# Gathered expert rows as whole rows of 8 KB in two buffers, with one VectorE operation of 2048 columns each, in place of half rows of 4 KB in three buffers

## The chip, the cores and the metric

One core of one Trainium2 chip runs the whole program. The metric is the device time of one execution in microseconds (us), the median over several runs. A profiled execution gives, besides its own time, the span from its first to its last instruction.

## What is computed

One block of a model over 256 tokens of width 2048, in fp32. A first half (RMSNorm, one input projection, differential attention and a gated MLP group, an output projection, residual) is not touched. The second half is a PEER expert layer: each token scores 16384 experts through product keys, keeps 16 of them for each of 8 heads, and sums their value rows with gated, activated weights. The reference, cut to what matters:

```python
def one_block(xb):                      # xb: (128 tokens, 2048)
    q = (xb @ w_q).reshape(T, 8, 2, 128)
    sc = jnp.einsum('thcd,hckd->thck', q, sub_keys)
    s1, i1 = lax.top_k(sc[:, :, 0], 16)
    s2, i2 = lax.top_k(sc[:, :, 1], 16)
    cand = (s1[..., :, None] + s2[..., None, :]).reshape(T, 8, 256)
    best, ci = lax.top_k(cand, 16)
    e1 = jnp.take_along_axis(i1, ci // 16, axis=-1)
    e2 = jnp.take_along_axis(i2, ci % 16, axis=-1)
    idx = e1 * 128 + e2                 # 128 picks per token
    g = jax.nn.softmax(best, axis=-1)
    act = jax.nn.gelu(jnp.einsum('td,thkd->thk', xb, u_tab[idx]))
    return jnp.einsum('thk,thkd->td', g * act, v_tab[idx])
```

`u_tab` and `v_tab` are two tables of 16384 rows of 2048 fp32 values, 8 KB a row.

## The kernel before

The expert layer is done in two ways at once. For 208 of the 256 tokens the kernel multiplies with both tables in full on TensorE: a **score stage** over `u_t` (128 steps of two units, 256 units of 512 KB each, called n below) and a **value stage** over `peer_v` (256 units, called v or u). In each unit ScalarE copies the loaded 512 KB into a rounded high part `HI` (L674), VectorE, or GpSimd in some plain steps, subtracts it from the raw data to get the low part (L1136 in the score stage, L445 on GpSimd, L1129 for two units at once in the value stage), and TensorE multiplies high with high and low (L1557, L1597) and low with high (L1563, L1602). TensorE's instructions for unit n are eight high products, then the eight low products of unit n-1. SyncE loads the units (L376) into a ring of 6 slots in the score stage and of 10 in the value stage; a slot is loaded again once the low products of the unit in it have been done.

The other 48 tokens are the **gathered tokens**. Each of their 48 x 128 picks is one row of `peer_u` and one of `peer_v`. With 128 picks on the 128 partitions, they make NG = 48 groups for each table: 32 groups for the first 32 tokens, 16 for the last 16. GpSimd fetches a group by an indirect DMA (L454) into a buffer `PICKED`, with the row numbers in `PK4`. VectorE then multiplies the rows with the tokens' input and sums them to one dot product per partition (L1190, with a small instruction that reads the accumulator), or in the value stage multiplies them by their weight and adds them to `ACC4` or `ACC8` (L1198, L1195 for the first). Each group is handled as two halves of 1024 columns, so there are 192 indirect DMAs and 192 VectorE operations. Three half buffers are in turn: gather k waits until VectorE has done operation k-3.

The order of the work is written out by hand, the same for all engines. What sets it around the change:

- In a score step j VectorE does, in this order: the sum of the two halves of PSUM (`sum_halves`, L1145), the low parts of units 2j+4 and 2j+5, some pieces of the choice of experts (top-k, one-hots and sums; `PIECE_COUNT`, up to step 56), from step 60 to 111 the one-hots and gates, and then a row operation if j is in the list `HALF_STEPS`. These are steps 40, 43, ..., 58, then every second step from 60 to 110, then every step from 112 to 120: 42 operations.
- In the value stage VectorE does for each even u the low part of the weights (L1205) and of two units of values (L1129), and a row operation if u is in `HALF_UNITS`: 150 operations on units 9 to 248, some 1.6 units apart.
- GpSimd goes through the same steps: a low part where one is its own, then the gathers that have become free. After the score stage it loads `X8` (L482) with the last 16 tokens' input, and late in the value stage it issues twelve loads for the end of the kernel (L492), one behind each gather.

GpSimd's row numbers come from VectorE: `SPK` is made from the picked experts (L1105 to L1108), saved to memory and read back as `PK4`. Since the halves are rows of a table of 32768 half rows, the number is doubled, and the second half's is that plus one:

```python
link(v.tensor_scalar(SPK[:, 0, :], SPK[:, 0, :], 1, None, ALU.logical_shift_left))
v.tensor_scalar(SPK[:, 1, :], SPK[:, 0, :], 1, None, ALU.bitwise_or)
```

Of the kernel before, what the change touches and what calls it, by code (L numbers as in the profile page):

```python
# [14 lines left out]
P = 128  # L15
# [35 lines left out]
ROW_SLOTS = 3  # L51
# [51 lines left out]
HALF_UNITS = [FREE_UNITS[i * len(FREE_UNITS) // (HALVES - len(HALF_STEPS))] for i in range(HALVES - len(HALF_STEPS))]  # L103
LAST_DOT = HALF_UNITS[2 * NG - 1 - len(HALF_STEPS)]
FIRST_B_DOT = HALF_UNITS[2 * GROUPS_A - len(HALF_STEPS)]
FIRST_B_SUM = HALF_UNITS[2 * NG + 2 * GROUPS_A - len(HALF_STEPS)]
SEL_A_AT = 2 * NKEYS - 4
assert 0 < FIRST_B_DOT and LAST_DOT < NKEYS - 1 and FIRST_B_SUM >= NKEYS + 62
GATHERED = {j: (ROW_SLOTS if j >= ROWS_BACK_AT else 0) + sum(i < j for i in HALF_STEPS) for j in range(NKEYS)}
# [25 lines left out]
def hybrid_peer_block(nc, x, w_in, w_out, wq_t, keys_t, u_t, peer_u, peer_v, ws_t, bs_t, gain_t, ffn_gain, z_gain,  # L135
                      final_gain, lambdas, rope, out):
    ctx = ExitStack()
    with ctx:  # L138
# [42 lines left out]
        SPK = at("SPK", 94 * KB, [P, 3, PICKS], U32)  # L181
# [25 lines left out]
        PICKED = [at("PICKED0", 192 * KB, [P, HALF]), at("PICKED1", 196 * KB, [P, HALF]), at("PICKED2", 104 * KB, [P, HALF])]  # L207
        PK4 = at("PK4", 108 * KB, [P, 3, NG], U32)
# [29 lines left out]
        DOTS = small("DOTS", [P, 2, NG])  # L238
# [5 lines left out]
        spk_dram = nc.dram_tensor("spk_spill", [NS, 3, PICKS], U32).ap()  # L244
# [43 lines left out]
        halves, dots, dots_gelu, sel_ready = sem("halves"), sem("dots"), sem("dots_gelu"), sem("sel_ready")  # L288
# [98 lines left out]
        def _(pool):  # L387
# [89 lines left out]
            for k in range(GATHERED[NKEYS - 1], len(HALF_STEPS) + ROW_SLOTS):  # L477
                gather(k)
# [8 lines left out]
            for k in range(len(HALF_STEPS) + ROW_SLOTS, HALVES):  # L487
                gather(k)
                if HALF_UNITS[k - ROW_SLOTS - len(HALF_STEPS)] >= NKEYS + 50 and late:
# [11 lines left out]
        def _(act):  # L501
# [258 lines left out]
            for v in range(N_V):  # L760
# [4 lines left out]
                if v == LAST_DOT:  # L765
                    act.wait_ge(dots, 1)
                    nc.scalar.activation(DOTS[:, 0, :], DOTS[:, 0, :], ACT.Gelu_apprx_tanh).then_inc(dots_gelu, 1)
# [31 lines left out]
        def _(dve):  # L799
# [260 lines left out]
            def choice(o):  # L1060
# [116 lines left out]
            def half_rows(k):  # L1177

                half = k % 2
                g = k % (2 * NG) // 2  # L1180
                cols = slice(half * HALF, (half + 1) * HALF)
                rows = PICKED[k % ROW_SLOTS][:]
                dve.wait_ge(row_ready[k % ROW_SLOTS], 16 * (k // ROW_SLOTS + 1))
                if k < 2 * NG:
                    if k == 0:
                        dve.wait_ge(x4_ready, 16 * (P // NA))
                    if k == 2 * GROUPS_A:
# [518 lines left out]
```

## Time and profile before

| | us |
|---|---|
| median of 3 runs | 1778.72 (1778.35 to 1779.86) |
| profiled execution, its own time | 1775.03 |
| its span, first to last instruction | 1772.9 |
| TensorE busy | 1743.1, 98% of the span |
| VectorE busy | 1424.3, 80% |
| ScalarE busy | 931.0, 53% |
| GpSimd busy | 410.6, 23% |
| granted TensorE clock, mean | 0.998 |

The score stage runs from 454 to 1129 us of the span, the value stage from 1130 to 1757 us. Busy times are unions of the instructions' durations; PE is TensorE's matmuls, PEld its weight loads, DVE is VectorE, ACT ScalarE, POOL GpSimd, SPq the queue of SyncE that issues loads. The idle time given in a row is that of the engine just before the instruction, with the instruction that ended it.

### The profile page before, as it was taken

To read this page: it belongs to the slowest core of one execution; us is meant where nothing else is said; L and a number is where in the kernel's file an instruction comes from. 1 tells how busy PE (TensorE), PEld (TensorE's weight loads), DVE (VectorE), ACT (ScalarE), POOL (GpSimd) and SP (SyncE) were. 2 spreads that over 40 slices of the span, in tenths; PEclk is the share of its full clock that TensorE was granted. 3 is DMA by queue.
4 is the path that set the end of the run, shared out by engine and by line. 5 is a ranking of instruction groups with operands and counts; after the bars stand their busy time and mean duration, and the time that the engine had idled before them with its cause. 6 is when DMAs were issued, how large, how long until landed. Compare 5 with 4: busy or idle time off the path is not lost. (4 is left out here: it accounts for less than half of the span.)

```text
span 1772.9 us, 28848 instructions
## 1 busy us (share of the span) xinstructions
PE 1743.1 (98%) x10950; PEld 1653.4 (93%) x10950; DVE 1424.3 (80%) x2151; ACT 931.0 (53%) x1400; POOL 410.6 (23%) x294
## 2 busy tenths in 40 slices
PE   9999999999999999999999999999999999999997
PEld 7887778778999999999999999999999999999997
DVE  5545786475579899999999998588888998888995
ACT  5444564453456554555555555555555555555553
POOL 0002300020142133111111112023433333343331
PEclk9999999999999999999999999999999999999999
DMA  7665445677566677777677778899999999999992
GB/s 245 210 183 161 143 148 170 193 234 237 175 219 218 218 256 243 248 244 228 227 231 231 233 233 314 256 335 367 353 359 356 354 321 356 365 363 405 368 349 91
DMA packets 127026, 462.59 MB, mean 261 GB/s; under 512 B 14736, under 2 KB 14832, under 8 KB 126240
## 3 DMA queue, kind: packets, MB, share of 16 engines
q1 hardware_dynamic: 95760, 347.65, 59.0%
q0 software_dynamic: 30992, 112.67, 17.1%
q8 instruction: 84, 1.38, 0.3%
q10 hardware_dynamic: 144, 0.52, 0.1%
q14 instruction: 46, 0.38, 0.1%
HBM read 455.73 MB, written 5.05 MB: 260 GB/s over the span
## 5 line engine op out<-in xcount | busy, mean ns | idle before, releaser
L1597 PE MATMUL PS<-W,HI 128*128 128x416 f32 x2048 | 436.9, 353 | 2.1 <-ACT HI L674 1.4
L1557 PE MATMUL PS<-xT,HI 128*128 128x416 f32 x2048 | 438.1, 356 | 0.0
L674 ACT ACTIVATE HI<-V_RAW 128x1024 fp32r<-128x1024 f32 x256 | 271.6, 1061 | 284.1 <-PE PS L1597 152.2
L1597 PEld LDWEIGHTS PS<-W,HI 128*128 128x128 f32 x2048 | 365.0, 189 | 7.2 <-ACT HI L674 1.6
L1557 PEld LDWEIGHTS PS<-xT,HI 128*128 128x128 f32 x2048 | 365.8, 189 | 2.3
L1129 DVE TENSOR_TENSOR V_LO<-V_RAW,HI 128x2048 fp32r<-128x2048 f32 x128 | 293.0, 2289 | 59.7 <-ACT HI L674 53.5
L674 ACT ACTIVATE HI<-RING_RAW 128x1024 fp32r<-128x1024 f32 x256 | 269.5, 1053 | 50.8 <-DMA RING_RAW<-u_t 49.7
L1136 DVE TENSOR_TENSOR RING_LO<-RING_RAW,HI 128x1024 fp32r<-128x1024 f32 x232 | 274.6, 1218 | 6.8 <-ACT HI L674 6.7
L811 DVE TENSOR_TENSOR LO<-RAW,HI 128x1024 fp32r<-128x1024 f32 x132 | 163.0, 1237 | 136.4 <-PE PS L1330 99.9
L1563 PEld LDWEIGHTS PS<-xT,RING_LO 128*128 128x128 f32 x2048 | 268.3, 191 | 4.1 <-DVE RING_LO L1136 2.0
L1602 PEld LDWEIGHTS PS<-W,V_LO 128*128 128x128 f32 x2048 | 269.3, 191 | 1.9 <-DVE V_LO L1129 0.9
L1602 PE MATMUL PS<-W,V_LO 128*128 128x208 f32 x2048 | 268.3, 272 | 0.5 <-DVE V_LO L1129 0.5
L1563 PE MATMUL PS<-xT,RING_LO 128*128 128x208 f32 x2048 | 266.9, 273 | 1.3 <-DVE RING_LO L1136 1.3
L454 POOL DMA_INDIRECT PICKED<-peer_u,PK x96 | 146.4, 1525 | 492.6 <-DVE DOTS L1190 484.3
L504 ACT ACTIVATE HI<-RAW 128x1024 fp32r<-128x1024 f32 x144 | 152.7, 1065 | 156.1 <-DMA RAW<-wq_t 47.4
L454 POOL DMA_INDIRECT PICKED<-peer_v,PK x96 | 134.5, 1401 | 234.3 <-DVE ACC L1198 202.6
L1325 PE MATMUL PS<-HI,xT 128*128 128x512 f32 x440 | 139.3, 398 | 2.5 <-ACT HI L504 1.8
L1330 PE MATMUL PS<-HI,xT 128*128 128x512 f32 x440 | 136.0, 390 | 0.0
L707 ACT ACTIVATE HOLES<-PS 128x208 f32<-128x208 f32 x128 | 44.1, 345 | 153.3 <-PE PS L1563 151.3
L1198 DVE SCALAR_TENSOR_TENSOR ACC<-PICKED,DOTS,ACC 128x1024 f32<-128x1024 f32 x92 | 116.5, 1279 | 9.2 <-DMA PICKED<-peer_v,PK 9.1
L1190 DVE CUSTOM_DVE_ANT_0 PICKED<-PICKED,X 128x1024 f32<-128x1024 f32 x96 | 116.4, 1219 | 6.6 <-DMA PICKED<-peer_u,PK 4.8
L1330 PEld LDWEIGHTS PS<-HI,xT 128*128 128x128 f32 x440 | 82.6, 188 | 17.6
(207 smaller groups left out, 1656.4 us busy)
## 6 DMA issues: line engine op xcount, KB each, us to landing
RING_RAW<-u_t SPq DMA_DIRECT2D x256, 512.0 KB
V_RAW<-peer_v SPq DMA_DIRECT2D x256, 512.0 KB
RAW<-w_in SPq DMA_DIRECT2D x80, 512.0 KB, 3.6
RAW<-w_out SPq DMA_DIRECT2D x32, 512.0 KB, 4.3
RAW<-wq_t SPq DMA_DIRECT2D x32, 512.0 KB, 4.8
x_spill<-X POOLq DMA_DIRECT2D x2, 1024.0 KB, 5.3
X1R<-x_spill POOLq DMA_DIRECT2D x8, 256.0 KB
X<-x SPq DMA_DIRECT2D x3, 512.0 KB, 8.4
```

The lines of the kernel that those rows point to most:

```text
L454: pool.indirect_dma_start(PICKED[k % ROW_SLOTS][:], None, table.rearrange("e (a c) -> (e a) c", a=2), bass.IndirectOffsetOnAxis(PK4[:, hal ...
L504: nc.scalar.activation(HI[:, slot, :], RAW[:, slot, :], ACT.Copy).then_inc(hi_ready, 1)
L674: nc.scalar.activation(HI[:, n % HI_SLOTS, :], raw_of(n), ACT.Copy).then_inc(top_ready, 1)
L811: v.tensor_tensor(LO[:, u % 2, :], RAW[:, u % 4, :], HI[:, u % 4, :].bitcast(FP32), ALU.subtract).then_inc(lo_ready[u % 2], 1)
L1129: nc.vector.tensor_tensor(pair_of(V_LO, v), pair_of(V_RAW, v), HI[:, slot:slot + 2, :].bitcast(FP32), ALU.subtract)\
L1136: v.tensor_tensor(low_of(n), raw_of(n), HI[:, n % HI_SLOTS, :].bitcast(FP32), ALU.subtract).then_inc(low_dve, 1)
L1325: mm(banks[c], high(tt), h[:, halves[c]], start=first, stop=False)
L1330: ins = mm(banks[c], low(tt), h[:, halves[c]], start=False, stop=last and tt > 0)
L1557: return mm(PS[:, j % S_BANKS, 0:2 * ND].rearrange("p (a t) -> p a t", a=2), HI[:, n % HI_SLOTS, kk * P:(kk + 1) * P], xT[:, k, :, 0:ND], ...
L1563: return mm(PS[:, j % S_BANKS, 0:ND], low_of(n)[:, kk * P:(kk + 1) * P], xT[:, k, 0, 0:ND], start=False, stop=k == KT - 1)
L1597: return mm(PS[:, V_BANKS[i], 0:2 * ND].rearrange("p (a t) -> p a t", a=2), HI[:, v % HI_SLOTS, i * P:(i + 1) * P], weights_of(v), start=v ...
L1602: return mm(PS[:, V_BANKS[i], 0:ND], low_of(N_U + v)[:, i * P:(i + 1) * P], weights_of(v)[:, 0, :], start=False, stop=v % NKEYS == NKEYS - 1)
```

## The change

A group's 128 rows are fetched whole, by one indirect DMA of 8 KB for each row. There are two buffers of 8 KB a partition instead of three of 4 KB, so gather k waits for operation k-2. A row operation works on 2048 columns; there are 96 of them and 96 gathers. `ROW_STEPS` are 40, 46, 52, 58, then every fourth step from 60 to 108, then 112, 114, ..., 120: 22 operations. `ROW_UNITS` are 74 units from 9 to 246, some 3.2 apart. The two instructions that double the row numbers go, and so does the addition of the two halves' dot products; `SPK` and `PK4` have two planes instead of three. The last operation on `peer_u` rows signals `dots` itself. In the value stage an operation adds to the accumulator that the operation before it wrote, so it waits for that one (`rows_done >= k`), where before it waited for the last but one.

```diff
-ROW_SLOTS = 3
+ROW_SLOTS = 2
...
-HALVES = 4 * NG
-HALF_STEPS = list(range(40, SPREAD0, 3)) + list(range(SPREAD0, SPREAD_END, 2)) + list(range(SPREAD_END, NKEYS - 7))
+ROW_STEPS = list(range(40, SPREAD0, 6)) + list(range(SPREAD0, SPREAD_END, 4)) + list(range(SPREAD_END, NKEYS - 7, 2))
...
-        PICKED = [at("PICKED0", 192 * KB, [P, HALF]), at("PICKED1", 196 * KB, [P, HALF]), at("PICKED2", 104 * KB, [P, HALF])]
-        PK4 = at("PK4", 108 * KB, [P, 3, NG], U32)
+        PICKED = [at("PICKED0", 192 * KB, [P, D]), at("PICKED1", 104 * KB, [P, D])]
...
             def gather(k):
 
-                table = peer_u if k < 2 * NG else peer_v
-                g, half = k % (2 * NG) // 2, k % 2
                 if k >= ROW_SLOTS:
-                    pool.wait_ge(halves, k - ROW_SLOTS + 1)
-                pool.indirect_dma_start(PICKED[k % ROW_SLOTS][:], None,
-                                        table.rearrange("e (a c) -> (e a) c", a=2),
-                                        bass.IndirectOffsetOnAxis(PK4[:, half, g:g + 1], 0))\
+                    pool.wait_ge(rows_done, k - ROW_SLOTS + 1)
+                pool.indirect_dma_start(PICKED[k % ROW_SLOTS][:], None, peer_u if k < NG else peer_v,
+                                        bass.IndirectOffsetOnAxis(PK4[:, 0, k % NG:k % NG + 1], 0))\
                     .then_inc(row_ready[k % ROW_SLOTS], 16)
...
-                    link(v.tensor_scalar(SPK[:, 0, :], SPK[:, 0, :], 1, None, ALU.logical_shift_left))
-                    v.tensor_scalar(SPK[:, 1, :], SPK[:, 0, :], 1, None, ALU.bitwise_or)
-                    v.tensor_copy(SPK[:, 2, :].bitcast(FP32), ROWS[:, 2]).then_inc(spk, 1)
+                    v.tensor_copy(SPK[:, 1, :].bitcast(FP32), ROWS[:, 2]).then_inc(spk, 1)
...
-            def half_rows(k):
+            def full_rows(k):
...
-                    ins = v.tensor_tensor_reduce(rows, rows, x_rows[:, cols], 1.0, 0.0, ALU.mult, ALU.add,
-                                                 DOTS[:, half, g:g + 1])
+                    ins = v.tensor_tensor_reduce(rows, rows, x_rows[:], 1.0, 0.0, ALU.mult, ALU.add, DOTS[:, g:g + 1])
...
-                        dve.wait_ge(halves, k - 1)
-                        ins = v.scalar_tensor_tensor(acc, rows, DOTS[:, 0, g:g + 1], acc, ALU.mult, ALU.add)
-                ins.then_inc(halves, 1)
+                        dve.wait_ge(rows_done, k)
+                        ins = v.scalar_tensor_tensor(acc, rows, DOTS[:, g:g + 1], acc, ALU.mult, ALU.add)
+                ins.then_inc(dots if k == NG - 1 else rows_done, 1)
...
-                        v.tensor_tensor(DOTS[:, 0, :], DOTS[:, 0, :], DOTS[:, 1, :], ALU.add).then_inc(dots, 1)
```

On VectorE's queue in score step 43 there stands a row operation before. The rows are its pieces of the choice (`CAND`, `BEST`), the row operation (`PICKED`), and the start of step 44. Before:

```order
L1057 MAX BEST<-CAND 128x8
L1058 MAX_INDEX CI<-BEST,CAND 128x8
L1190 ISA PICKED_101,DOTS<-PICKED_101,X_95 128x1024
L1190 ISA DOTS 128x1
L1145 TENSOR_TENSOR store<-PS,HOLES 128x208
L1136 TENSOR_TENSOR RING_LO<-RING_RAW,HI 128x1024
```

Now, in the same place:

```order
L1051 MAX_INDEX CI<-BEST,CAND 128x8
L1052 MATCH_REPLACE CAND<-BEST,CAND 128x256
L1053 MAX BEST<-CAND 128x8
L1054 MAX_INDEX CI<-BEST,CAND 128x8
L1139 TENSOR_TENSOR store<-PS,HOLES 128x208
L1130 TENSOR_TENSOR RING_LO<-RING_RAW,HI 128x1024
```

The half row operation of step 43 is gone; steps 49 and 55 lose theirs in the same way.

At the end of score step 46 and the start of step 47, VectorE before:

```order
L1089 CAST CF<-CIA 128x128
L1190 ISA PICKED_102,DOTS<-PICKED_102,X_95 128x1024
L1190 ISA DOTS 128x1
L1145 TENSOR_TENSOR store<-PS,HOLES 128x208
L1136 TENSOR_TENSOR RING_LO<-RING_RAW,HI 128x1024 x2
```

Now:

```order
L1085 CAST CF<-CIA 128x128
L1182 ISA PICKED_101,DOTS<-PICKED_101,X_95 128x2048
L1182 ISA DOTS 128x1
L1139 TENSOR_TENSOR store<-PS,HOLES 128x208
L1130 TENSOR_TENSOR RING_LO<-RING_RAW,HI 128x1024 x2
```

The operation in this place has twice the columns, and it is the second of the stage where it was the third; steps 40, 52 and 58 change likewise.

## Rows read from the trace of the kernel before

**Rows 1.** The page, part 1: busy us, share of the span, instructions

```profile
PE 1743.1 (98%) x10950; PEld 1653.4 (93%) x10950; DVE 1424.3 (80%) x2151; ACT 931.0 (53%) x1400; POOL 410.6 (23%) x294
```

**Rows 2.** Waits of PEld, 454 to 1773 us: total us, times, longest us

```profile
PEld PS L1563 <- DVE RING_LO L1136: 2.0, 2, 1.1
PEld PS L1597 <- ACT HI L674: 1.6, 1, 1.6
...
PEld PS L1602 <- DVE V_LO L1129: 0.9, 1, 0.9
```

**Rows 3.** Timeline of PEld, 680 to 710 us: start us, us, what [idle before]

```profile
689.00 1.44 PEld L1557 LDWEIGHTS PS<-xT,HI 128*128 128x128 f32 x8
...
691.41 1.44 PEld L1557 LDWEIGHTS PS<-xT,HI 128*128 128x128 f32 x8
693.91 0.97 PEld L1563 LDWEIGHTS PS<-xT,RING_LO 128*128 128x128 f32 x8 [1.07 <-DVE RING_LO L1136]
...
702.10 1.44 PEld L1557 LDWEIGHTS PS<-xT,HI 128*128 128x128 f32 x8
704.50 0.97 PEld L1563 LDWEIGHTS PS<-xT,RING_LO 128*128 128x128 f32 x8 [0.96 <-DVE RING_LO L1136]
```

**Rows 4.** Window 692 to 703 us: us, then PE, PEld, DVE, ACT, POOL busy

```profile
692.00:703.00 11.00, 10.29 (x68) 9.74 (x67) 10.62 (x28) 5.01 (x8) 2.40 (x1) 1.00 0.74 251
```

**Rows 5.** The page, part 5: groups, count | busy us, mean ns | idle before

```profile
L1129 DVE TENSOR_TENSOR V_LO<-V_RAW,HI 128x2048 fp32r<-128x2048 f32 x128 | 293.0, 2289 | 59.7 <-ACT HI L674 53.5
...
L454 POOL DMA_INDIRECT PICKED<-peer_u,PK x96 | 146.4, 1525 | 492.6 <-DVE DOTS L1190 484.3
...
L1198 DVE SCALAR_TENSOR_TENSOR ACC<-PICKED,DOTS,ACC 128x1024 f32<-128x1024 f32 x92 | 116.5, 1279 | 9.2 <-DMA PICKED<-peer_v,PK 9.1
L1190 DVE CUSTOM_DVE_ANT_0 PICKED<-PICKED,X 128x1024 f32<-128x1024 f32 x96 | 116.4, 1219 | 6.6 <-DMA PICKED<-peer_u,PK 4.8
```

**Rows 6.** Timeline of DVE near 685 and 1340 us

```profile
685.00 1.28 DVE L1190 CUSTOM_DVE_ANT_0 PICKED<-PICKED,X 128x1024 f32<-128x1024 f32 x1
...
686.20 0.36 DVE L1145 TENSOR_TENSOR store<-PS,HOLES 128x208 f32<-128x208 f32 x1
...
1339.06 2.29 DVE L1129 TENSOR_TENSOR V_LO<-V_RAW,HI 128x2048 fp32r<-128x2048 f32 x1
1341.26 1.22 DVE L1190 CUSTOM_DVE_ANT_0 PICKED<-PICKED,X 128x1024 f32<-128x1024 f32 x1
...
1342.40 0.58 DVE L1205 TENSOR_TENSOR W<-store,W 128x416 fp32r<-128x416 f32 x1
```

**Rows 7.** Timelines of POOL, SP, ACT and PEld, 1103 to 1120 us

```profile
1103.36 1.96 POOL L454 DMA_INDIRECT PICKED<-peer_u,PK  x1 [4.89 <-DVE DOTS L1190]
...
1104.82 0.33 SPq L376 DMA_DIRECT2D RING_RAW<-u_t  x1
...
1112.07 1.06 ACT L674 ACTIVATE HI<-RING_RAW 128x1024 fp32r<-128x1024 f32 x1 [2.97 <-DMA RING_RAW<-u_t]
...
1119.36 1.06 ACT L674 ACTIVATE HI<-RING_RAW 128x1024 fp32r<-128x1024 f32 x1 [0.91 <-DMA RING_RAW<-u_t]
...
1114.18 1.44 PEld L1557 LDWEIGHTS PS<-xT,HI 128*128 128x128 f32 x8
```

**Rows 8.** Window 1109 to 1110 us: ..., PEclk, DMA share, GB/s

```profile
1109.00:1110.00 1.00, 1.00 (x9) 1.00 (x8) 1.00 (x2) 0.10 (x1) 0.00 (x0) 1.00 1.00 393
```

**Rows 9.** Timeline of DVE, 1606 to 1622 us

```profile
1609.08 1.28 DVE L1198 SCALAR_TENSOR_TENSOR ACC<-PICKED,DOTS,ACC 128x1024 f32<-128x1024 f32 x1 [1.28 <-DMA PICKED<-peer_v,PK]
1612.96 1.29 DVE L1198 SCALAR_TENSOR_TENSOR ACC<-PICKED,DOTS,ACC 128x1024 f32<-128x1024 f32 x1 [2.59 <-DMA PICKED<-peer_v,PK]
```

**Rows 10.** Timeline of DVE near 615 and 808 us: two sums and their idle time

```profile
614.61 0.38 DVE L1145 TENSOR_TENSOR store<-PS,HOLES 128x208 f32<-128x208 f32 x1 [0.80 <-ACT HOLES L707]
...
807.73 0.38 DVE L1145 TENSOR_TENSOR TMP<-PS,HOLES 128x208 f32<-128x208 f32 x1 [0.63 <-ACT HOLES L707]
```

**Rows 11.** Timeline of PEld, 1142 to 1152 us

```profile
1147.27 1.44 PEld L1597 LDWEIGHTS PS<-W,HI 128*128 128x128 f32 x8 [1.59 <-ACT HI L674]
```

More of the change, by code:

```diff
@@ L96 @@
 PIECE_COUNT, PLAIN_STEP = piece_counts()
-HALVES = 4 * NG
-HALF_STEPS = list(range(40, SPREAD0, 3)) + list(range(SPREAD0, SPREAD_END, 2)) + list(range(SPREAD_END, NKEYS - 7))
+ROW_STEPS = list(range(40, SPREAD0, 6)) + list(range(SPREAD0, SPREAD_END, 4)) + list(range(SPREAD_END, NKEYS - 7, 2))
 FREE_UNITS = [u for u in range(9, 250) if u not in (NKEYS - 2, NKEYS - 1)]
[L103 to L106, printed above, removed]
+ROW_UNITS = [FREE_UNITS[i * len(FREE_UNITS) // (2 * NG - len(ROW_STEPS))] for i in range(2 * NG - len(ROW_STEPS))]
+LAST_DOT = ROW_UNITS[NG - 1 - len(ROW_STEPS)]
+FIRST_B_DOT = ROW_UNITS[GROUPS_A - len(ROW_STEPS)]
+FIRST_B_SUM = ROW_UNITS[NG + GROUPS_A - len(ROW_STEPS)]
 SEL_A_AT = 2 * NKEYS - 4
 assert 0 < FIRST_B_DOT and LAST_DOT < NKEYS - 1 and FIRST_B_SUM >= NKEYS + 62
-GATHERED = {j: (ROW_SLOTS if j >= ROWS_BACK_AT else 0) + sum(i < j for i in HALF_STEPS) for j in range(NKEYS)}
+GATHERED = {j: (ROW_SLOTS if j >= ROWS_BACK_AT else 0) + sum(i < j for i in ROW_STEPS) for j in range(NKEYS)}
 S_BANKS = 3
@@ L180, in hybrid_peer_block @@
         ROWS = at("ROWS", 92 * KB, [P, 3, PH * TOPK])
-        SPK = at("SPK", 94 * KB, [P, 3, PICKS], U32)
+        SPK = at("SPK", 94 * KB, [P, 2, PICKS], U32)
         KEYS = at("KEYS", 96 * KB, [P, HC, NKEYS])
@@ L237, in hybrid_peer_block @@
         TMP = small("TMP", [P, ND])
-        DOTS = small("DOTS", [P, 2, NG])
+        DOTS = small("DOTS", [P, NG])
+        PK4 = small("PK4", [P, 2, NG], U32)
         PS = ctx.enter_context(nc.psum_tensor("PS", [P, 8, BANK], FP32))
@@ L476, in _ @@
                     gather(k)
-            for k in range(GATHERED[NKEYS - 1], len(HALF_STEPS) + ROW_SLOTS):
+            for k in range(GATHERED[NKEYS - 1], len(ROW_STEPS) + ROW_SLOTS):
                 gather(k)
@@ L486, in _ @@
                      for c in range(D // BANK)]
-            for k in range(len(HALF_STEPS) + ROW_SLOTS, HALVES):
+            for k in range(len(ROW_STEPS) + ROW_SLOTS, 2 * NG):
                 gather(k)
-                if HALF_UNITS[k - ROW_SLOTS - len(HALF_STEPS)] >= NKEYS + 50 and late:
+                if ROW_UNITS[k - ROW_SLOTS - len(ROW_STEPS)] >= NKEYS + 50 and late:
                     pool.wait_ge(low_used, N_U + NKEYS + 44)
@@ L1175, in land @@
                 v.tensor_tensor(store[:, j, 0:t], store[:, j, 0:t], TMP[:, 0:t], ALU.mult).then_inc(landed, 1)
[L1177 to L1181 removed]
+            def full_rows(k):
+                g = k % NG
                 rows = PICKED[k % ROW_SLOTS][:]
                 dve.wait_ge(row_ready[k % ROW_SLOTS], 16 * (k // ROW_SLOTS + 1))
[L1184 removed]
+                if k < NG:
                     if k == 0:
                         dve.wait_ge(x4_ready, 16 * (P // NA))
[L1187 removed]
+                    if k == GROUPS_A:
                         dve.wait_ge(x8_ready, 16 * (P // NB_))
                     x_rows = X4 if g < GROUPS_A else X8
[L1190 to L1191 removed]
+                    ins = v.tensor_tensor_reduce(rows, rows, x_rows[:], 1.0, 0.0, ALU.mult, ALU.add, DOTS[:, g:g + 1])
                 else:
[L1193 removed]
+                    acc = (ACC4 if g < GROUPS_A else ACC8)[:]
                     if g in (0, GROUPS_A):
[L1195 removed]
+                        ins = v.tensor_scalar(acc, rows, DOTS[:, g:g + 1], None, ALU.mult)
                     else:
[L1197 to L1199 removed]
+                        dve.wait_ge(rows_done, k)
+                        ins = v.scalar_tensor_tensor(acc, rows, DOTS[:, g:g + 1], acc, ALU.mult, ALU.add)
+                ins.then_inc(dots if k == NG - 1 else rows_done, 1)
+                if k == NG - 1:
+                    dve.wait_ge(dots, 1)
+                    dve.sem_inc(rows_done, 1)
             def weights_lo(q):
@@ L1629, in last_unit @@
                         if i == 0:
-                            pe.wait_ge(halves, HALVES)
+                            pe.wait_ge(rows_done, 2 * NG)
                         ins = gathered_out(i, ACC8, SEL8, NA, NB_, True)
@@ L1657, in _ @@
                     pe.wait_ge(sel_ready, 2)
-                    pe.wait_ge(halves, HALVES - 2 * GROUPS_B)
+                    pe.wait_ge(rows_done, 2 * NG - GROUPS_B)
                     for i in range(DT):
```

24 lines of the change are left out of this document (10 added, 14 removed).

## The prediction, made before the changed kernel ran

> **What bounds the kernel.** I read the page's busy times first, then the waits of TensorE's weight loads in the two expert stages, then the timelines at the places where it waits. TensorE is busy for 98% of the span, VectorE for 80% [rows 1]. TensorE's weight loads come in units of 2.41 us, one unit starting at 689.00 and the next at 691.41 [rows 3]. What another engine costs the kernel is only what makes a unit longer, and there is little of that: 2.0 us in two waits for VectorE's `RING_LO` in the score stage, 1.6 us in one wait for ScalarE's `HI` and 0.9 us in one wait for `V_LO` at the start of the value stage [rows 2]. At 691.41 the eight high products start; they take 1.44 us, so the low ones should start at 692.85, and start at 693.91 [rows 3]. The other wait, at 704.50, is of the same kind and 0.96 us long. Around these two VectorE has no room: 10.62 us busy of 11 [rows 4]. They are in score steps 45 and 47, where the pieces of the choice and the row operations both lie.
>
> So the change can win at most 2.0 us in the score stage, plus the 2.5 us of waits in the value stage if those are its doing. It can lose wherever it makes VectorE or a load late by more than its margin.
>
> **VectorE's work.** A half row operation shows as 1219 ns on `peer_u` and 1279 ns on `peer_v`, and there are 192 of them with the four first ones [rows 5]. What counts is the distance from its start to the next start: 1.20 us at 685.00, 1.14 us at 1341.26 [rows 6]. A whole row operation is not in the trace. The nearest row is `V_LO`, two inputs and 2048 columns in fp32: 2289 ns [rows 5], 2.20 us from start to start [rows 6]. From below, nothing makes it less than one half (1.14); from above, it is at most two halves (2.3 to 2.4). I take 2.2, from the row with its very shape, for both kinds. The 96 pairs then shrink by about 0.1 us each, some 9 us of VectorE's time in all. Nearly all of it is worth nothing, since VectorE ends most steps by waiting for ScalarE or TensorE, as for 0.63 us at 807.73 in the gated steps and 0.80 us at 614.61 [rows 10], and in the value stage for `HI`, 53.5 us in sum [rows 5].
>
> **Where the lumps fall.** In steps 40 to 58 the half operations at 40, 43, 46 and so on become whole ones at 40, 46, 52, 58. Up to step 43's end VectorE is 2.2 - 1.15 = 1.05 us later than before, after it 0.1 us earlier. Up to the second stall (step 47) three half operations have run before (3.5 us, the 1.20 one included) and two whole ones now (4.4 us): VectorE is 0.9 us later just where TensorE already waited for it. VectorE has no idle time between to take this up [rows 4]. The waits therefore add up to 2.0 + 0.9 = 2.9 us instead of 2.0. Earlier, the 1.05 us meets small margins in steps 41 to 44 and makes a wait there; that is part of the 2.9 us and not added to it, since each wait moves TensorE back and gives VectorE time for the next. Once TensorE has slipped by 0.9 us, the later lumps (steps 52 and 58) put VectorE no later against it than before. **Term 1: +0.9 us.** Its bounds are -2.0 us, if the waits vanish, and +1.3 us, if a whole operation costs two halves.
>
> **Loads of the ring.** A gather now moves 1 MB at once instead of 512 KB, in the same bytes overall. In steps 112 to 120 this meets the ring of six slots. The unit whose load SyncE issues at 1104.82 is copied by ScalarE at 1112.07, 7.25 us later, after 2.97 us idle; a gather was issued at 1103.36. The copy is done at 1113.13 and TensorE starts on the unit at 1114.18, so 1.05 us were left [rows 7]. A later unit with no gather before it made ScalarE idle for 0.91 us [rows 7]. One gather of 512 KB so costs a load up to 2.06 us. The other 512 KB, if they move at the 393 GB/s of the busiest slice there [rows 8], take 1.3 us; less the margin of 1.05 us, 0.3 us of wait remain for that unit. There are five such gathers (after the operations of steps 112 to 120), and for most the margin is larger. From below this costs nothing (the gather and the load need not meet). From above each of the five costs 2.06 us more, 1.0 us over the margin, 5 us in sum. **Term 2: +0.5 us**, by the rate of the busiest slice, one or two gathers of the five.
>
> The Trainium skill's page "DMA: Bandwidth & Descriptors", section "Queues, rings and completion order", says that each DMA engine goes round the queues packet by packet and empties a whole packet, some 9 to 17 descriptors, before it turns to the next queue. With 8 rows of each gather on an engine that would let a load wait for a whole gather, now of twice the length, which is the first rival below. This trace has only the 2.06 us of one half gather.
>
> **GpSimd.** 96 indirect DMAs of about 1.5 us [rows 5] go, with as many waits. GpSimd had waited for VectorE for 484 us before them [rows 5], so nobody gains. Its low parts in steps 41 to 45 wait for VectorE's and move with term 1; the gather of step 44 no longer stands behind one of them. **Other edits**, each at nothing: the two instructions on `SPK` (about half a us) lie in step 30, and VectorE waits for `HOLES` in the next step [rows 10]; without that wait they would be worth their own length. The addition of the dot products is one small operation in the value stage, where VectorE has room. The wait for the operation just before the accumulation is free, as the two are some 3 units (7 us) apart. The twelve late loads go out over more units, end near unit 214 instead of 197, and are needed behind unit 255.
>
> **Value stage.** A pair of units lasts 4.8 us. With a whole row operation VectorE needs 2.2 for `V_LO`, 0.5 for the weights and 2.2 for the rows, 4.9 us, and in the pairs without one 2.7. It lags by 0.1 us and has it back in the next pair. Its margin there is large: near 1609 it lost 1.28 and 2.59 us in waiting for two gathers [rows 9], and no wait of TensorE answers to it [rows 2]. Two buffers of whole rows also give a gather more time, two intervals of 3.2 units against three of 1.6. The one wait of 1.59 us at 1147.27 [rows 11] falls before the first row operation of that stage, with no row gather under way, and behind the burst of `X8` and ring loads, so it stays. **Term 3: 0.**
>
> **Sum.** The profiled execution took 1775.03 us, 3.69 us under the median of 1778.72. Against its own time the change gives 1775.03 + 0.9 + 0.5 + 0 = 1776.4; against the median **1780.1 us**, 0.08% slower. A difference under 0.2% (3.6 us) can't be told from no change here.
>
> **Rivals.**
> 1. *Slower: each whole gather holds back a load of the ring by twice the time.* For it: 2.97 us idle against 0.91, and 1.05 us left [rows 7]. Against it: in most of the score stage VectorE, not the load, sets when a unit is ready. It decides once a gather costs a load over 3.1 us (2.06 + 1.05). At twice 2.06 us, five gathers cost 5 us: 1778.7 + 0.9 + 5.0 = 1784.7 us. Chance 16%.
> 2. *Faster: VectorE's stalls go.* If a whole operation costs much less than 2.2 us, or the lumps fall where they do no harm, the 2.0 us of [rows 2] go: 1776.7 us, still within 0.2%. With the 2.5 us at the start of the value stage as well, 1774.2 us. Against it: the row of 2048 columns takes its full time [rows 5]. Chance 8%, of which 3% for the second.
> 3. *VectorE becomes late in the value stage*, since a whole operation behind a late gather keeps it from `V_LO`. Longest wait for a gather now 2.59 us [rows 9]; doubled and with 1.1 us more of operation this comes to 6.3 us, about the margin; two such places would cost 2 us: 1782 us. Chance 5%.
> 4. *The change moves nothing*: 8 KB rows travel as two 4 KB pieces, the lumps are taken up. 1778.7 us. Chance 11%.
>
> My forecast has 60%. Its own range is 1779 to 1782. The range for 8 in 10 takes in rival 4 and most of rivals 1 and 2, up to the bounds of term 2: 1777.0 to 1784.0. Faster by over 0.2% (under 1775.2) comes only from the second half of rival 2: 3%. Slower by over 0.2% (over 1782.3) comes from rival 1 (14%) and a part of rival 3 (2%): 16%. Within: 81%.
>
> **What would show it.** Right: row operations near 2.3 us long, and a count of 96; TensorE waiting for `RING_LO` two to four times in score steps 41 to 47, 2.9 us in sum; units of 2.41 us everywhere else; the wait near 1147 as it was; ScalarE idle for up to 4 us before some `HI` in steps 112 to 125, and TensorE waiting for `HI` there for under 1 us. Rival 1 shows as waits of TensorE for `HI` of about 1 us behind each of the gathers in steps 113 to 121. The forecast is wrong if `RING_LO` waits stay at 2.0 us or fall, if the value stage shows waits for `V_LO` past its first ten units, or if units become longer without any wait.

## The result, and the profile after

The changed kernel takes **1789.77 us**, the median of 5 runs (1785.48 to 1793.76), beside 1778.72 us before on the same chip: ratio 1.0055, 95% interval 1.004 to 1.007 (the two medians alone give 1.0062). It is slower by 0.55%. The forecast of 1780.1 us was wrong, and so was its range (1777.0 to 1784.0). A second set of runs gave 1788.89 us, ratio 1.0067 (1.0051 to 1.0084). The profiled execution took 1785.48 us, with a span of 1783.7 us; the span before was 1772.9 us. So 10.8 us have to be found.

The page after, busy times and DMA queues:

```profile
span 1783.7 us, 28557 instructions
...
PE 1746.9 (98%) x10950; PEld 1654.9 (93%) x10950; DVE 1413.8 (79%) x2004; ACT 930.5 (52%) x1400; POOL 259.2 (15%) x198
...
DMA packets 113201, 462.52 MB, mean 259 GB/s; under 512 B 13201, under 2 KB 13297, under 8 KB 100129
...
q1 hardware_dynamic: 95760, 347.65, 60.0%
q0 software_dynamic: 17168, 112.61, 16.9%
```

TensorE's share is as before [rows 1], and VectorE has some 10 us less to do. A whole row did become one packet of 8 KB: 113201 less 100129 packets are of 8 KB or more. Queue 0, which carries the gathers, now holds its engines for 0.169 x 16 x 1783.7 / 17168 = 0.28 us a packet on average, small ones included.

The two row operations after (groups of instructions, shapes kept apart: count, busy us, mean ns, idle before):

```profile
L1182 DVE CUSTOM_DVE_ANT_0 PICKED<-PICKED,X 128x2048 f32<-128x2048 f32 x48 | 109.7, 2285 | 0.6 <-DMA PICKED<-peer_u,PK 0.5
L1189 DVE SCALAR_TENSOR_TENSOR ACC<-PICKED,DOTS,ACC 128x2048 f32<-128x2048 f32 x46 | 107.9, 2347 | 3.6 <-DMA PICKED<-peer_v,PK 3.6
```

The one on `peer_u` is as long as the row of 2048 columns that was taken for them (2289 ns) [rows 5], the one on `peer_v` 58 ns longer, and VectorE waits for gathers for 4.1 us in all. The waits of TensorE's weight loads in the two expert stages after (engine, tile and line, what was waited for: us in total, times, longest):

```profile
PEld PS L1588 <- issue: 2.8, 2, 2.2
PEld PS L1554 <- DVE RING_LO L1130: 2.5, 3, 2.0
PEld PS L1588 <- DVE OUTA L1233: 2.1, 7, 0.3
PEld PS L1548 <- ACT HI L670: 1.3, 3, 0.7
PEld PS L1538 <- ACT SC L688: 0.9, 1, 0.9
PEld PS L1593 <- DVE V_LO L1123: 0.8, 1, 0.8
PEld PS L1518 <- DVE HOLES L1151: 0.8, 2, 0.6
```

Against [rows 2] there is 0.5 us more for `RING_LO`, and new waits: for `HI` in the score stage (L1548), for the one-hots (`HOLES`), 0.7 us more for `OUTA` (1.4 us before). The wait of 2.2 us put down to "issue" is at the start of the value stage, where before there was the wait of 1.6 us for `HI`; it ends at 1154.47, as the weights `W` are done at 1154.43. These are a few us, not ten. The rest is at two places that a list of waits in the stages does not show. The first is the end of the program; the waits of SyncE's queue after, from 1760 us on:

```profile
SPq L137 <- PEq L137: 4.8, 1, 4.8
SPq L137 <- DMA out<-X1R: 2.7, 1, 2.7
```

And the last work on GpSimd and ScalarE after, from the timelines (start us, us, what, idle before):

```profile
1770.57 3.29 POOL L493 TENSOR_TENSOR X1R<-X1R,FG 128x1024 f32<-128x1024 f32 x1 [0.52 <-ACT FJ L520]
...
1773.96 1.15 ACT L779 ACTIVATE X1R<-X1R,SS 128x1024 f32<-128x1024 f32 x1 [0.91 <-POOL X1R L493]
```

The last computing instruction ends at 1775.11, and the stores of `out` are down 2.7 us after the last is issued. SyncE then waits 4.8 us more for the other engines (in the kernel before the same last wait is 0.2 us). The one that is late is GpSimd. The last instruction of its program but two short semaphore events is a drain (L137). It is issued at 1770.54, beside its last multiplication, and ends at 1783.43 in the trace, 9.6 us behind that multiplication. In the kernel before it ends at 1772.01, 4.3 us behind.

The second place is TensorE's clock. Its timeline after, behind the matmuls with `SEL` that sum the gathered tokens, and the window of its wait-free stretch (us, then PE, PEld, DVE, ACT, POOL busy, PEclk, DMA share, GB/s):

```profile
1746.99 3.71 PE L1601 MATMUL PS<-SEL,ACC 128*128 128x32 f32 x32
1750.52 3.12 PE L1588 MATMUL PS<-W,HI 128*128 128x416 f32 x8
...
1754.54 1.67 PE L1588 MATMUL PS<-W,HI 128*128 128x416 f32 x8
```

```profile
1750.50:1753.90 3.40, 3.40 (x13) 3.27 (x13) 0.00 (x0) 0.00 (x0) 0.00 (x0) 0.50 0.00 0
```

The granted clock is 0.50 there, the lower of the two levels, 1.2 GHz: eight high products take 3.12 us. In the kernel before the same eight took 1.75 us:

```profile
1745.96 1.75 PE L1597 MATMUL PS<-W,HI 128*128 128x416 f32 x8
```

### The profile page after: what moved, and what is told of

It is laid out like the page before. It is cut to its first block and busy times, and to the rows that moved or that the text cites. A ratio compares the mean times of both kernels' runs of the same rounds, so it can differ in the third digit from the quotient of the medians.

```text
span 1783.7 us, 28557 instructions
## 1 busy us (share of the span) xinstructions
PE 1746.9 (98%) x10950; PEld 1654.9 (93%) x10950; DVE 1413.8 (79%) x2004; ACT 930.5 (52%) x1400; POOL 259.2 (15%) x198
## 2 busy tenths in 40 slices
DMA packets 113201, 462.52 MB, mean 259 GB/s; under 512 B 13201, under 2 KB 13297, under 8 KB 100129
## 3 DMA queue, kind: packets, MB, share of 16 engines
q0 software_dynamic: 17168, 112.61, 16.9%
## 5 line engine op out<-in xcount | busy, mean ns | idle before, releaser
L1548 PE MATMUL PS<-xT,HI 128*128 128x416 f32 x2048 | 438.7, 356 | 0.8 <-ACT HI L670 0.8
L1548 PEld LDWEIGHTS PS<-xT,HI 128*128 128x128 f32 x2048 | 365.9, 189 | 4.1 <-ACT HI L670 1.3
L451 POOL DMA_INDIRECT PICKED<-peer_u,PK x48 | 68.4, 1424 | 557.2 <-DVE DOTS L1182 552.5
L1189 DVE SCALAR_TENSOR_TENSOR ACC<-PICKED,DOTS,ACC 128x2048 f32<-128x2048 f32 x46 | 107.9, 2347 | 3.6 <-DMA PICKED<-peer_v,PK 3.6
L1182 DVE CUSTOM_DVE_ANT_0 PICKED<-PICKED,X 128x2048 f32<-128x2048 f32 x48 | 109.7, 2285 | 0.6 <-DMA PICKED<-peer_u,PK 0.5
L451 POOL DMA_INDIRECT PICKED<-peer_v,PK x48 | 61.9, 1290 | 316.4 <-DVE ACC L1189 291.6
```

What stands on the lines that cost most here:

```text
L451: pool.indirect_dma_start(PICKED[k % ROW_SLOTS][:], None, peer_u if k < NG else peer_v, bass.IndirectOffsetOnAxis(PK4[:, 0, k % NG:k % NG ...
L1548: return mm(PS[:, j % S_BANKS, 0:2 * ND].rearrange("p (a t) -> p a t", a=2), HI[:, n % HI_SLOTS, kk * P:(kk + 1) * P], xT[:, k, :, 0:ND], ...
```

## The experiments

Theory: three costs are separate, the lumps of whole operations on VectorE, the rows of 8 KB, and whatever makes the end long. Main rival: all of it comes from the coarser gathers of 1 MB.

**Halved gathers, whole operations.** The changed kernel, each 8 KB buffer filled by two gathers of 4 KB rows back to back:

```diff
-pool.indirect_dma_start(PICKED[k % ROW_SLOTS][:], None, peer_u if k < NG else peer_v, ...)
+for half in range(2):
+    pool.indirect_dma_start(PICKED[k % ROW_SLOTS][:, half * HALF:(half + 1) * HALF], None,
+                            table.rearrange("e (a c) -> (e a) c", a=2), ...)
```

> The changed kernel, but each whole buffer is filled by two indirect DMAs of 4 KB rows, one right behind the other; VectorE's order is the changed one. Theory A (the lumps of VectorE cost the time): as the changed kernel within 2 us, with 2.9 us of waits for RING_LO near 684 to 706 us and the waits of TensorE near 1150 and 1445 us unchanged. Theory B (rows of 8 KB, one long packet each, hold back other loads or the end of GpSimd): within 2 us of the kernel before, and GpSimd's last drain ends before the output's stores again, which gives back some 5 us. Theory C (the end of GpSimd is an accident of one execution): that drain is short or long here whatever the gathers.

Measured: 1779.27 us, ratio 1.0015 (1.0004 to 1.0025). Waits of TensorE's weight loads, and of SyncE at the end:

```profile
PEld PS L1559 <- DVE RING_LO L1135: 2.4, 2, 1.6
PEld PS L1593 <- issue: 2.2, 2, 1.6
PEld PS L1593 <- DVE OUTA L1238: 2.1, 7, 0.3
PEld PS L1543 <- ACT SC L691: 1.3, 1, 1.3
PEld PS L1559 <- POOL RING_LO L444: 1.0, 1, 1.0
```

```profile
SPq L137 <- PEq L137: 0.2, 1, 0.2
```

The `RING_LO` waits are here (3.4 us) and the longer boundary (`OUTA`) too, but no wait for `HI` or the one-hots, no long end, and the clock is whole behind `SEL`. Whole operations alone cost 0.15%, some 2.7 us. This is theory B of the expectation; theory A, that the lumps on VectorE cost all of it, is out.

**Whole gathers, half operations.** The 96 gathers of 1 MB stay, VectorE works in halves at the places of the kernel before:

```diff
-ROW_STEPS = list(range(40, SPREAD0, 6)) + list(range(SPREAD0, SPREAD_END, 4)) + ...
+HALF_STEPS = list(range(40, SPREAD0, 3)) + list(range(SPREAD0, SPREAD_END, 2)) + ...
...
-rows = PICKED[k % ROW_SLOTS][:]
+rows = PICKED[full % ROW_SLOTS][:, cols]
```

> Whole rows gathered into two buffers as in the changed kernel, but VectorE works on halves at the places of the kernel before. Theory A: waits for RING_LO back to 2.0 us, no waits for the one-hots near 777 us, flush near 1445 us as before; 3 to 4 us faster than the changed kernel in the stages. Theory B: within 2 us of the changed kernel, with its long drain of GpSimd at the end and its waits for HI near 1078 us.

Measured: 1804.46 us, ratio 1.0146 (1.0125 to 1.0167). VectorE's waits for gathers, and TensorE's answer:

```profile
DVE ACC L1194 <- DMA PICKED<-peer_v,PK: 64.6, 23, 5.0
DVE PICKED L1186 <- DMA PICKED<-peer_u,PK: 15.3, 12, 2.2
```

```profile
PEld PS L1593 <- issue: 20.7, 10, 5.1
```

Neither theory held, and this does not measure what it was made for. A buffer is free only after its second half operation, and its next rows are wanted after three half intervals; the gathers come too late for that. In VectorE's order the weights `W` stand behind the row operation, and TensorE's matmuls wait for `W` 12.9 us in nine waits between 1160 and 1760 us. (The profiled execution was the longest of the four, 1814.4 us.) The kernel needs the whole operations to give a gather of 1 MB its time. The long end (4.8 us) is here too.

**The changed kernel and the one before, again.** No edit.

> The changed kernel again, for a second profile. If the 4.7 us at the end (GpSimd's last drain, 1770.5 to 1783.4 us) and the 3.4 us of half clock near 1750 us belong to the change, both are here again; if they are accidents, at least one is gone and the profiled time is 1.5 to 5 us shorter. The stalls near 684 to 706 us should be 2.9 us again to within 0.3 us.

> The kernel before again, for a second profile and as a test of the timing: ratio 1.000 to within 0.002. GpSimd's last drain ends at about 1772 us as before if its length belongs to the kernel, and may end later by some 5 us if it is an accident.

Measured: 1788.89 us (ratio 1.0067) and 1777.50 us (ratio 1.0003, 0.9993 to 1.0013). The profile after repeats its main points: SyncE's last wait of 4.8 us, the half clock for 3.4 us behind `SEL`, and waits for `HI` in the score stage, now 3.3 us. The one before has a last wait of 0.2 us and no half clock there.

**Short rows.** 96 gathers, of the first 4 KB of each row only:

```diff
-pool.indirect_dma_start(PICKED[k % ROW_SLOTS][:], None, peer_u if k < NG else peer_v, ...)
+pool.indirect_dma_start(PICKED[k % ROW_SLOTS][:, 0:HALF], None,
+                        table.rearrange("e (a c) -> (e a) c", a=2), ...)
```

The second half of each buffer is set to zero once and stays so; this kernel leaves out half of every gathered row.

> The changed kernel with its 96 gathers of 128 rows, but of only the first 4 KB of each row; the second half of each buffer stays zero, and the operations still run over 2048 columns. It leaves out the second half of every gathered row, so half the gathered bytes. It asks whether the length of a row (8 KB) or the number of gathers (96) makes what the halved gathers did not show. Theory A (the 8 KB rows): GpSimd's last drain is back at about 4 us, no half clock behind the SEL matmuls, no waits for ring loads; only the VectorE lumps stay (+2 us), so 1779 us, ratio 1.001. Rival B (96 gathers instead of 192, whatever their length): the drain stays at 9.6 us and the time is at least 1784 us, ratio 1.004.

Measured: 1785.33 us, ratio 1.0036 (1.0022 to 1.005): rival B, as far as the end goes. No wait for `HI` is left in the score stage, so those belong to the 8 KB rows or the doubled bytes of a gather. But the end is as long as ever with half the bytes and short rows, and the clock is again at half behind `SEL`:

```profile
SPq L137 <- PEq L137: 4.8, 1, 4.8
```

**Split gathers.** 192 gathers of 64 rows of 8 KB:

```diff
+for q in range(2):
+    part = slice(64 * q, 64 * q + 64)
+    pool.indirect_dma_start(PICKED[k % ROW_SLOTS][part, :], None, ...,
+                            bass.IndirectOffsetOnAxis(PK4[0:64, 2 * q, ...], 0))
```

> The changed kernel with each buffer filled by two gathers of 64 rows of 8 KB back to back (partitions 0 to 63, then 64 to 127): 192 gathers as before, 8 KB rows, the same bytes; 12 small loads of indices more at step 35. Theory A (the 8 KB rows): as the changed kernel, drain about 9.6 us, half clock behind the SEL matmuls, 1786 to 1790 us, ratio 1.005 to 1.007. Rival B (the number of gathers, or 1 MB at one go): drain about 4 us and 1779 us, ratio 1.001, as with the halved gathers.

Measured: 1964.11 us, ratio 1.1028 (1.1002 to 1.1053), which neither theory expected. The end is short again (SyncE's last wait 0.2 us), with 8 KB rows; so the end goes with the number of gathers. The 185 us more are something else. The median from issue to landing between 1600 and 1700 us is 10.6 us here, and 10.6 us in the changed kernel with moved operations (below), which gathers 128 rows. The first fence is this kernel's, the second that one's (issues: count, KB where it is told, median us to landing):

```profile
PICKED<-peer_v,PK POOLq DMA_INDIRECT x21, 10.6
```

```profile
PICKED<-peer_v,PK POOLq DMA_INDIRECT x12, 10.6
```

The two figures do not mean that 64 rows take as long as 128, since the two gathers of a buffer overlap: by the trace the first lands 9.5 us after its issue, the second 11.5 us after its own, and the buffer is full 12.8 us after the first issue (medians), against 10.6 us with one gather. A row of 8 KB holds its DMA engine for 564 ns here (median of its packets) and for 309 ns in the changed kernel.

By the page, which averages over all packets of the gathers' queue, it holds its engines for 0.240 x 16 x 1967.0 / 18896 = 0.40 us a packet, where it was 0.28 us:

```profile
q0 software_dynamic: 18896, 112.63, 24.0%
```

So loads of units come late: ScalarE waits 400.2 us in 169 waits for loads of the value stage, where it waited 63.4 us in the changed kernel. TensorE waits for `HI` (24.9 us in 14 waits in the score stage), and in the value stage its matmuls wait for the weights `W` (67.8 us in 47). Its granted clock is 0.970 in the mean, so a part of the 185 us is the clock. Why a packet to half the partitions takes longer is not settled. The Trainium skill's page "DMA: Bandwidth & Descriptors", section "Why a DMA increments its semaphore by 16 and not by 1", spreads a transfer over the largest number of engines up to 16 that divides its slowest dimension on both sides. With rows as that dimension, 64 rows go over all 16 as 128 do, so by that rule the number of engines is no reason for the longer packets; no run here shows it.

**Moved operations.** The kernel of the first experiment (4 KB rows), with the row operations of steps 40, 46, 52 and of units 120 to 131 moved to other units:

```diff
-ROW_STEPS = list(range(40, SPREAD0, 6)) + ...
-FREE_UNITS = [u for u in range(9, 250) if u not in (NKEYS - 2, NKEYS - 1)]
+ROW_STEPS = [58] + ...
+FREE_UNITS = [u for u in range(9, 250) if not NKEYS - 8 <= u < NKEYS + 4]
```

> The kernel with 4 KB gathers into whole buffers and whole operations (1779.3 us), with its whole operations taken out of score steps 40, 46 and 52 and out of units 120 to 131 around the half boundary, to other units of the value stage. Theory (the lumps of 2.3 us on VectorE cost only where VectorE is already full): the RING_LO waits of steps 40 to 58 go from 3.3 us of excess to under 1, and the boundary of the halves from 2.8 back to 1.8, so about 1776 us, ratio 0.9985 or lower, below both kernels. Rival (the lumps are not it; the waits there come from the packing of VectorE's other work): RING_LO waits stay at 2 us or more and the time at 1778 to 1779 us.

The same edit on the changed kernel:

> The changed kernel with the same whole operations moved as in the run before. If lumps and 8 KB rows are separate costs that add: about 3 us less than the changed kernel, 1785 to 1786 us, ratio 1.004, with the drain at 9.6 us and the half clock behind the SEL matmuls still there. If the drain or the half clock follow from where the operations lie instead, one of them is gone and the time is 1781 us or less.

And the same on the kernel before, with its half operations:

> The kernel before (halves, three 4 KB buffers) with its half operations taken out of steps 40 to 57 and of units 120 to 131, to other steps and units of the value stage. If VectorE's load in those steps makes the RING_LO waits, they go from 1.9 us to about 0 here too, and the time falls by 1.5 to 2 us, ratio 0.999. If not, 1778 us as before, ratio 1.000.

Measured: 1779.20 us, ratio 1.0013 (0.9992 to 1.0033); 1787.82 us, ratio 1.0047 (1.0031 to 1.0062); 1780.62 us, ratio 1.0017 (1.0003 to 1.003). In none of the three profiles is a wait for `RING_LO` left: the mechanism behind term 1 is shown. The time is not won, though. In the kernel before with moved operations, TensorE waits in the value stage instead (1.6 us for `HI` in the kernel before [rows 2], and 0.8 us of "issue"):

```profile
PEld PS L1597 <- ACT HI L674: 4.6, 4, 1.4
PEld PS L1597 <- issue: 2.9, 4, 1.8
```

The name `HI` in this list misleads in three of the four waits; only the one near 1147 us, at the start of the stage, is for `HI`. ScalarE's waits for loads between 1160 and 1740 us are short, 1.3 us in all (8.8 us in the kernel before). What TensorE waits for there is `W`. Its matmuls in that stretch say so in the first line; the second and third are VectorE's timeline and the fourth PEld's at one of the four places:

```profile
PE PS L1597 <- DVE W L1205: 4.7, 4, 1.7
```

```profile
1610.59 1.28 DVE L1198 SCALAR_TENSOR_TENSOR ACC<-PICKED,DOTS,ACC 128x1024 f32<-128x1024 f32 x1 [3.03 <-DMA PICKED<-peer_v,PK]
1611.79 0.58 DVE L1205 TENSOR_TENSOR W<-store,W 128x416 fp32r<-128x416 f32 x1
```

```profile
1612.49 0.68 PEld L1597 LDWEIGHTS PS<-W,HI 128*128 128x128 f32 x4 [1.30 <-ACT HI L674]
```

VectorE waits 3.03 us for a gather, `W` stands behind that row operation and ends at 1612.37, and TensorE goes on at 1612.49, 1.3 us late. `HI` was done at 1611.64. So with the row operations closer together in the value stage, gathers come late and hold back `W`. The time went up by 2.9 us (median 1780.62 beside 1777.73 us) where 2.0 us were to be won. The same is seen at two places of halved gathers with moved operations, and it is rival 3 of the prediction with `W` in the place of `V_LO`. In the changed kernel with moved operations ScalarE also waits for loads of the value ring at the two places of this kind, 1.65 us before 1646.71 and 2.27 us before 1670.95. The changed kernel itself has no wait for `W` between the start of the value stage and 1740 us.

**The end of GpSimd's program.** The changed kernel with the two last multiplications by the final gain on VectorE:

```diff
-nc.gpsimd.tensor_tensor(X1R[:, tt, 0:HALF], X1R[:, tt, 0:HALF], FG[:, 0:HALF], ALU.mult).then_inc(gained, 1)
+v.tensor_tensor(X1R[:, tt, 0:HALF], X1R[:, tt, 0:HALF], FG[:, 0:HALF], ALU.mult).then_inc(gained, 1)
```

> The changed kernel with the two last multiplications by the final gain on VectorE and not on GpSimd, so that GpSimd's program ends behind its last loads, at about 1736 us of the span. Theory (the end of GpSimd's program takes 9.6 us with this kernel, and it is the last thing that ends): that end now runs beside other work, SyncE's last wait for the other engines is back at 0.2 us, and the time falls by 4 to 5 us, to about 1784 to 1785 us, ratio 1.003 to 1.004. Rival (something later than the last store holds the end, wherever the multiplications are): the time stays at 1788 to 1790 us.

The changed kernel with a small gather behind each of its own:

```diff
+if k:
+    pool.wait_ge(extra, 16 * k)
+pool.indirect_dma_start(EX[0:2, :], None, peer_u.rearrange("e (a c) -> (e a) c", a=32),
+                        bass.IndirectOffsetOnAxis(PK4[0:2, 0, k % NG:k % NG + 1], 0))
```

> The changed kernel with a second, small gather (2 rows of 256 bytes, to a place that nothing reads) behind each of its 96 gathers: 192 gathers, and all else as in the changed kernel. Theory (GpSimd's long last drain comes with the number of gathers: 96 long, 192 short): the last multiplication of GpSimd to the end of its drain is 3 to 4.5 us, SyncE's last wait 0.2 us, and the time 4 to 5 us under the changed kernel, 1784 to 1785 us. Rival (it comes with buffers filled by one gather, whatever else is issued): the drain stays at 9.6 us and the time at 1788 us or more.

Measured: 1786.00 us, ratio 1.0049 (1.003 to 1.0067), and 1784.16 us, ratio 1.0039 (1.0024 to 1.0053). SyncE's last waits, with the multiplications on VectorE, and then with the small gathers:

```profile
SPq L137 <- DMA out<-X1R: 2.9, 1, 2.9
SPq L137 <- PEq L137: 0.2, 1, 0.2
```

```profile
SPq L137 <- DMA out<-X1R: 2.6, 1, 2.6
...
SPq L137 <- PEq L137: 0.2, 1, 0.2
```

In both SyncE's last wait is 4.6 us shorter. In the first, GpSimd's drain is 15.8 us long in the trace, from 1730.02 to 1745.85, and nobody waits for it. In the second, 96 gathers were added and 5 us of time went: the closing drain ends at 1776.42, 2.8 us behind the last multiplication (its row: 1770.34 and 3.30 us). The added gathers also make GpSimd wait for the landing of each small one, so more than the count was changed. The time of the second is as expected. The time of the first is 1 us above what was expected, and its interval overlaps that of the changed kernel (1.0051 to 1.0084 in the second set), so the 4.6 us are shown there by the trace and not by the time. Its profiled execution shows what else lies in it: three waits for `HI` in the score stage, 2.5 us, and half clock at 1451 us as well as behind `SEL`.

**Both edits.** The changed kernel with moved operations and the multiplications on VectorE:

> The changed kernel with both edits, the whole operations moved out of the crowded steps and the last multiplications on VectorE: what is left is what the 8 KB rows cost elsewhere. If the costs add, 1787.8 us less 4.7, about 1783 us, ratio 1.002 to 1.003, still above the kernel before because of waits for ring loads beside 8 KB rows (some 3 to 4 us in the trace). If these waits were only a consequence of the others, 1779 us or less.

Measured: 1782.37 us, ratio 1.0024 (1.0015 to 1.0034), as expected if the costs add. It is the best kernel that gathers rows of 8 KB, and still slower than the one before. What is left shows in its waits:

```profile
PEld PS L1550 <- ACT HI L666: 3.1, 4, 1.2
PEld PS L1590 <- issue: 2.6, 5, 0.9
PEld PS L1590 <- ACT HI L666: 2.4, 2, 1.7
```

No version that was run beats the kernel before.

## Why the prediction was wrong, by its own steps

The step that failed most is the one on GpSimd: fewer gathers were put at nothing, "so nobody gains", and the runs showed 4.6 us at the end of the program. Next comes term 2, sized at 0.5 us and found at 2.6 to 4.7 us in the two profiles. Term 3, put at 0, is 1.0 us at the boundary of the halves. 1.4 us are a half clock that was in no term.

**Right: what bounds the kernel, and the size of a row operation.** Whole operations of 2.2 us from start to start, 96 of them; VectorE's saved time is worth nothing.

**Term 1 (+0.9 us) was right in place and size.** The prediction gave 2.9 us of waits for `RING_LO` in steps 41 to 47. The longest after is 2.0 us, in this stretch of the timelines of PEld and DVE, with the whole operation that VectorE does first:

```profile
702.03 2.29 DVE L1182 CUSTOM_DVE_ANT_0 PICKED<-PICKED,X 128x2048 f32<-128x2048 f32 x1
...
704.53 2.35 DVE L1130 TENSOR_TENSOR RING_LO<-RING_RAW,HI 128x1024 fp32r<-128x1024 f32 x2
```

All of them make 2.5 and 3.4 us of waits in the two profiles after, and 2.6 us of longer units in the first profile after and some 3.3 us in the second, against 1.9 and 2.1 us before. With the operations moved away they are 0.

**Term 2 (+0.5 us) failed in place and size.** It looked for loads held back in steps 112 to 120 only, where the ring was known to be tight. The first place where it happened is around step 37, behind the first two gathers, which are issued back to back, 2 MB in all, before any row operation. Timelines after:

```profile
633.91 1.03 POOL L451 DMA_INDIRECT PICKED<-peer_u,PK  x1 [4.26 <-DMA PK<-spk_spill]
635.25 1.98 POOL L451 DMA_INDIRECT PICKED<-peer_u,PK  x1 [0.30 <-issue]
```

```profile
645.01 1.06 ACT L670 ACTIVATE HI<-RING_RAW 128x1024 fp32r<-128x1024 f32 x1 [3.40 <-DMA RING_RAW<-u_t]
```

TensorE waits 0.45 us for this `HI` at 646.12 here, and the two units there are 2.8 us longer in the second profile. The next is in the late steps as forecast, but larger: ScalarE waits for a load for 5.05 us where "up to 4 us" was expected, and TensorE for 0.69 us:

```profile
1077.48 1.06 ACT L670 ACTIVATE HI<-RING_RAW 128x1024 fp32r<-128x1024 f32 x1 [5.05 <-DMA RING_RAW<-u_t]
```

In all, ScalarE's waits for ring loads in the score stage grew from 45.2 us to 62.8 us. That sum alone says little: it is 65.7 us in the kernel before with moved operations, where TensorE waits for no `HI` in that stage. Counted as longer units, loads and one-hots cost the score stage 2.6 us in the first profile after and 4.7 us in the second, 2.6 to 4.3 us in the three others with 8 KB rows and one or both late edits, and some 6 us with moved whole operations (4.4 us of it are waits for `HI`). This is rival 1 in kind, with 2 us or more of it at places that it did not name. The page "DMA: Bandwidth & Descriptors" of the Trainium skill, section "Queues, rings and completion order", says that a DMA engine takes a whole packet from one queue before it turns to the next. No run here shows the turn-taking itself. What fits it: with rows of 8 KB the queue's mean packet holds an engine for 0.28 us against 0.171 x 16 x 1772.9 / 30992 = 0.16 us before, and with 4 KB rows the waits for `HI` in the score stage are gone in halved gathers and short rows. They are not quite gone in halved gathers with moved operations, which has two, 1.1 us in all.

**Term 3 (0) missed the middle of the stage.** At the boundary of the two halves of the value matrix, units 125 to 129, VectorE has `V_LO`, the weights and the sums of `OUTA` to do in a row. A whole operation now stands in unit 125 where a half one stood. VectorE's timeline after:

```profile
1439.25 2.28 DVE L1123 TENSOR_TENSOR V_LO<-V_RAW,HI 128x2048 fp32r<-128x2048 f32 x1
1441.45 2.34 DVE L1189 SCALAR_TENSOR_TENSOR ACC<-PICKED,DOTS,ACC 128x2048 f32<-128x2048 f32 x1
1443.71 0.58 DVE L1199 TENSOR_TENSOR W<-store,W 128x416 fp32r<-128x416 f32 x1
1444.21 4.06 DVE L1233 TENSOR_REDUCE OUTA<-PS 128x208 f32<-128x416 f32 x8
```

The three units there lose 2.8 us instead of 1.8 us, and 1.0 us with the operations moved. The argument with "4.9 us of 4.8" took every pair of units to be alike; this one is not. The waits at the start of the stage make 2.6 and 2.1 us of longer units in the two profiles before, 3.0 and 3.6 us in the two after, and 1.7 us with halved gathers. The other profiles with gathers of 8 KB rows and whole operations have 1.8 to 3.7 us there, and halved gathers with moved operations 3.0 us. The forecast had them unchanged; they may have grown by 1 us, and these profiles don't settle it.

**What was not in the sum at all.** The end of the program, 4.6 us: the 96 indirect DMAs fewer were costed at nothing, "so nobody gains", because GpSimd had waited for VectorE before them. That argument covers GpSimd's work in the stages and not its closing drain, and that fewer gathers could lengthen the drain was in no row of before. The half clock behind `SEL`, 1.4 us (3.12 against 1.75 us); whether it belongs to the change is not settled (see the last section). These two make over half of the 10.8 us. (Rival 1's sum of 1784.7 us comes to 1784.6.)

**The sum as measured.** By ratios of the runs, in parts of 1778 us: whole operations 2.7 us (halved gathers, 1.0015); whole gathers of 8 KB rows 4.3 us more (small gathers, 1.0039); the number of gathers 3.9 us more (mean of the two sets of the changed kernel, 1.0061). Each ratio is uncertain by some 2 to 3 us either way, so the parts are by some 3 us; only the last one is also seen directly, as 4.6 us. The half clock behind `SEL` lies in the second part, since the small gathers have it and the halved gathers do not. "The change moves nothing" (rival 4) is out, so is rival 2, since the waits grew, and so is rival 3 for this kernel: no wait for `V_LO` past the start of the value stage.

## What to carry to other kernels

Here the engine that issues the gathers was idle anyway, so fewer and larger transfers gained nothing; they only made the steps coarser that a tight ring and a full engine have to absorb. Expect the same where the issuing engine is idle. Before doubling a unit of work, look at every place where the pattern of the stage breaks (its first transfer, its boundary, its last step), and not at the average pair. And look at how the program ends: an engine that has long stopped working can hold the end with its drain, and giving its last instruction to another engine shows it. When a list of waits names an engine, see in the timeline whether that engine had been done before: `HI` stood for `W` in the kernel before with moved operations.

## What the runs showed of the hardware

- GpSimd's closing drain ended 9.6 us behind its last multiplication in all five profiles with 96 gathers and the multiplications on it (the two of the changed kernel, half operations, short rows, moved whole), whatever the row length. It ended 2.7 to 4.7 us behind in all seven with 192 (the two before, halved gathers, split gathers, the two moved versions with halves, small gathers). So in these kernels the drain is shorter with more gathers. Why is open: no run tells whether the count itself matters or something that goes with it (the small gathers came with a wait for each landing), and no number between 96 and 192 was tried.
- TensorE's clock fell to 1.2 GHz behind the first 32 small `SEL` matmuls in 7 of the 8 profiles in which a buffer of 8 KB is filled by one gather (the two of the changed kernel, half operations, short rows, multiplications on VectorE, small gathers, both edits; not moved whole). It fell there in none of the 6 others (the two before, halved gathers, split gathers, the two moved versions with halves). It follows neither the row length nor the long drain. Falls at other places come and go between executions of one kernel: the second profile of the kernel before has a granted clock of 0.50 from 365.8 to 369.2 us, the first has none there. So the link with the gathers is a count of profiles and not a cause shown; the cause is open.
- Two gathers of 64 rows of 8 KB into one buffer, issued back to back, fill it 12.8 us after the first issue; one gather of 128 rows does it in 10.6 us (medians, 1600 to 1700 us). A packet of 8 KB takes 564 ns in the first case and 309 ns in the second.
